# Two value projections of a fused two-block kernel in one fill of 512 weight columns each, with the packed convolution and two transposes moved around the first of them

## The reference

```python
h = rmsnorm(x, mix_pre_norm[i])
u = h @ w_in[i]
...
hv = u[..., c1 + 2 * D_RET:c1 + 3 * D_RET]
...
y_conv = conformer_conv(u_a, u_b, conv_dw_w[i], conv_dw_b[i], conv_ln_w[i], conv_ln_b[i])
y_ret = retention_group(hq, hk, hv, hg)
```

```python
kv = (mem_n @ w_kv).reshape(b, m, 2, CA_HEADS, CA_DIM)
s = jnp.einsum('bthd,bmhd->bhtm', q, kv[:, :, 0]).astype(jnp.float32)
...
o = jnp.einsum('bhtm,bmhd->bthd', p, kv[:, :, 1]).reshape(b, t, CA_WIDTH)
```

## Time and profile before

| | |
|---|---|
| median of 3 runs | 904.84 us (904.33 to 904.93) |
| profiled execution, its own time | 903.12 us |
| its span in the trace | 901.2 us |
| TensorE busy | 888.2 us, 99% of the span |
| VectorE busy | 624.2 us, 69% |
| ScalarE busy | 502.9 us, 56% |
| GpSimd busy | 347.5 us, 39% |
| granted TensorE clock, mean | 0.999 |

### The profile page before, as it was taken

One profiled execution on the slowest core, in us unless ns is written; L12 is line 12 of the kernel. 1 busy time (PEld: TensorE's weight loads), 2 busy tenths in 40 slices (PEclk: granted clock), 3 DMA queues, 4 the chain that ended last, 5 costly groups with the idle time before them and its releaser, 6 DMA issues.

```text
span 901.2 us, 15285 instructions
## 1 busy us (share of the span) xinstructions
PE 888.2 (99%) x6308; PEld 780.8 (87%) x6308; DVE 624.2 (69%) x812; ACT 502.9 (56%) x730; POOL 347.5 (39%) x133
## 2 busy tenths in 40 slices
PE   8999999999999999999999999999999999999997
PEld 7999877888888878999999988877788888888886
DVE  6999757888882267668799765753415689999623
ACT  7545646444454356655566565555545576666533
POOL 2981002666664400000000008546783166666542
PEclk9999999999999999999999999999999999999999
DMA  9762645555556545545545534444464465555551
GB/s 356 259 213 95 236 149 209 189 187 187 187 188 208 204 149 187 187 152 179 199 135 183 179 87 179 159 163 149 140 210 140 159 232 192 188 188 187 186 187 47
DMA packets 31014, 162.44 MB, mean 180 GB/s; under 512 B 9154, under 2 KB 10322, under 8 KB 12514
## 3 DMA queue, kind: packets, MB, share of 16 engines
q1 hardware_dynamic: 30738, 161.13, 51.8%
q10 hardware_dynamic: 144, 0.26, 0.1%
q0 software_dynamic: 64, 0.08, 0.0%
HBM read 160.20 MB, written 1.27 MB: 179 GB/s over the span
## 4 chain that ended last, share of the span: by engine, by line
PE 84%; DVE 9%; ACT 3%; DMA 2%; issue 1%; POOL 1%; SPq 0%; DVEq 0%; ACTq 0%
PE acc L1874 18%; PE ring L1739 15%; PE ring L2228 12%; PE ring L1773 9%; PE acc L1773 9%; PE ring L1777 5%; PE ring L1820 4%; PE acc L1777 4%; DVE acc L1281 4%; DMA raw<-wstream 2%; PE acc L2083 1%; PE acc L1887 1%; ACT w_hi L728 1%; DVE rope_b L1315 1%; DVE w_lo L1164 1%
## 5 line engine op out<-in xcount | busy, mean ns | idle before, releaser
L728 ACT CAST w_hi<-raw 128x1024 fp32r<-128x1024 f32 x284 | 297.1, 1052 | 315.4 <-PE ring L1739 78.0
L674 POOL TENSOR_TENSOR w_lo<-raw,w_hi 128x1024 fp32r<-128x1024 f32 x118 | 331.8, 2816 | 313.1 <-ACT w_hi L728 312.9
L1164 DVE TENSOR_TENSOR w_lo<-raw,w_hi 128x1024 fp32r<-128x1024 f32 x166 | 214.3, 1300 | 112.2 <-ACT w_hi L728 102.8
L1739 PE MATMUL ring<-h,w_hi 128*128 128x256 f32 x960 | 174.3, 284 | 1.0 <-issue 1.0
L1739 PEld LDWEIGHTS ring<-h,w_hi 128*128 128x128 f32 x960 | 149.8, 192 | 1.0 <-issue 0.7
L1739 PE MATMUL ring<-h,w_lo 128*128 128x256 f32 x480 | 136.1, 283 | 0.0
L1739 PEld LDWEIGHTS ring<-h,w_lo 128*128 128x128 f32 x480 | 92.2, 192 | 1.1 <-issue 1.1
L699 POOL TENSOR_SCALAR_AFFINE_SELECT toep_t<-toep_t 64x2304 f32<-64x2304 f32 x2 | 5.9, 2938 | 224.1 <-DMA toep_t<-toep 224.0
L1874 PE MATMUL acc<-w_hi,ff 128*128 128x512 f32 x340 | 91.2, 390 | 0.0
L1773 PE MATMUL ring<-h,w_hi 128*128 128x512 f32 x352 | 88.2, 393 | 0.0
L1773 PE MATMUL acc<-h,w_hi 128*128 128x512 f32 x336 | 84.6, 394 | 0.0
(11 more groups left out here) (292 smaller groups left out, 1372.2 us busy)
## 6 DMA issues: line engine op xcount, KB each, us to landing
raw<-wstream SPq DMA_DIRECT2D x142, 1024.0 KB, 4.9
toep_t<-toep SPq DMA_DIRECT2D x16, 96.0 KB, 3.1
x<-x_tok SPq DMA_DIRECT2D x2, 512.0 KB, 4.5
mem<-mem_tok SPq DMA_DIRECT2D x1, 1024.0 KB, 11.2
w_ple<-wproj SPq DMA_DIRECT2D x1, 1024.0 KB, 7.2
decay<-decay_tab SPq DMA_DIRECT2D x1, 768.0 KB, 6.4
out_t<-y SPq DMA_DIRECT2D x3, 256.0 KB, 2.1
u<-uconv SPq DMA_DIRECT2D x4, 142.0 KB, 5.8
```

What stands on the lines that cost most here:

```text
L674: nc.gpsimd.tensor_tensor(w_lo[:, u % UNITS], unit_of_raw(u), as_f32(w_hi[:, u % UNITS]), ALU.subtract).then_inc(lo_ready["pool"], 1)
L728: nc.scalar.copy(w_hi[:, u % UNITS], unit_of_raw(u)).then_inc(hi_ready, 1)
L1164: V.tensor_tensor(w_lo[:, u % UNITS], unit_of_raw(u), as_f32(w_hi[:, u % UNITS]), ALU.subtract).then_inc(lo_ready["dve"], 1)
L1739: last = mm(dst, w[a], src[:, b, kt], start=n == 0 and i == 0, stop=n == kts - 1 and i == 2)
```

## The change

Both value projections become one fill of two banks. `token_rows` takes one token tile per bank and streams 512 weight columns per matmul; the order over (token tile, k tile) is tile 0 with k 0 to 3, tile 1 with k 0 to 3, and from k 4 on both tiles for each k. The host lays the weights out by rows of four blocks for it. At the first place the packed convolution moves ahead of `v`, both memory transposes stand behind `v`, one on each side of the mean, and POOL makes `w_conv` one unit earlier. ACT reads both banks of a fill together, with one signal. At the second place the four transposes stand ahead of (0, 7) and (1, 7), and ACT reads both banks behind the transposes' casts. The number of weights, units and DMA transfers stays.

```diff
-    ("v", 0, 1, 16, "act"), ("mem_x", 0, 1, 0, "dve"), ("v", 1, 1, 16, "act"), ("mem_x", 1, 1, 0, "dve"),
+    ("v", 0, 1, 32, "act"), ("mem_x", 0, 2, 0, "dve"),
...
-    ("ple", 0, 1, 64, "acc"), ("memv", 0, 2, 16, "act"), ("ple_x", 0, 4, 0, "dve"),
+    ("ple", 0, 1, 64, "acc"), ("memv", 0, 1, 32, "act"), ("ple_x", 0, 4, 0, "dve"),
...
-    return (PJ + 1 + j,) if name == "ple_x" else (RING.index(n) % PJ,)
+    if name == "ple_x":
+        return (PJ + 1 + j,)
+    slot = sum(2 if FILLS[m][0] in ROWS else 1 for m in RING if m < n)
+    return (slot % PJ, (slot + 1) % PJ) if name in ROWS else (slot % PJ,)
...
-            feed(end_unit("v", 0))
+            feed(first_unit("v") + 1)
             pool.wait_ge(load_params, 32)
...
-            copy_fill("v", 0, v_ret[:, :, 0:256])
             for i, t in enumerate(PACKED):
                 act.wait_ge(packed_conv, i + 1)
                 A(conv_y[:, t], sc[t][:, 0:S], ACT.Identity, bias=col("dw_b", t)).then_inc(packed_out, 1)
             prime(ACT.Sqrt)
 
+            wait_fill("v", 0)
+            for tt, src in enumerate(row_banks("v", 0)):
+                ins = nc.scalar.copy(v_ret[:, tt], src)
+            ins.then_inc(freed["act"], 1)
             turned_hi("mem", 0)
-            copy_fill("v", 1, v_ret[:, :, 256:512])
             turned_hi("mem", 1)
...
-            def memv_out(j):
-                act.wait_ge(pe_step, fill_step(fi("memv", j)))
-                nc.scalar.copy(mem_v[:, :, 256 * j:256 * j + 256], bank("memv", j)[:]).then_inc(freed["act"], 1)
+            def memv_out():
+                act.wait_ge(pe_step, fill_step(fi("memv", 0)))
+                for tt, src in enumerate(row_banks("memv", 0)):
+                    ins = nc.scalar.copy(mem_v[:, tt], src)
+                ins.then_inc(freed["act"], 1)
...
-            memv_out(0)
             turned_hi("ple", 0)
             turned_hi("ple", 1)
             feed_next("ple", 5)
             turned_hi("ple", 2)
             turned_hi("ple", 3)
             feed_next("ple", 6)
-            memv_out(1)
+            memv_out()
...
+            def token_rows(name, j, src, between=None):
+
+                banks = row_banks(name, j)
+                n = fi(name, j)
+                held = {b: m for m in earlier_fills(n) for b in filled_banks(m)}
+                first = at_block[0] // UB
+                order = [(tt, kt) for tt in range(2) for kt in range(4)]
+                order += [(tt, kt) for kt in range(4, KT) for tt in range(2)]
+                for tt, kt in order:
+                    u, c = first + kt // 2, 4 * (kt % 2)
+                    if between is not None and (tt, kt) in between:
+                        between[tt, kt]()
+                    if kt == 0:
+                        m = held[filled_banks(n)[tt]]
+                        pe.wait_ge(freed[FILLS[m][3]], freed_count(m, FILLS[m][3]))
+                    if tt == 0 and c == 0:
+                        pe.wait_ge(lo_ready[LO_ENGINE[u]], lo_count(u, LO_ENGINE[u]))
+                    for part, w in ((0, w_hi), (0, w_lo), (1, w_hi)):
+                        last = mm(banks[tt], src[:, part, kt, tt * P:tt * P + P],
+                                  w[:, u % UNITS, c:c + 4].rearrange("p a b -> p (a b)"),
+                                  start=kt == 0 and part == 0 and w is w_hi, stop=kt == KT - 1 and part == 1)
+                    if tt == 1 and c:
+                        at_block[0] += UB
+                        step(last, at_block[0])
...
-            token_pair("v", 0, h)
             pe.wait_ge(w_conv_ready, len(PACKED))
             pe.wait_ge(conv_loaded, 16 * TAPS)
             for i, t in enumerate(PACKED):
                 conv_packed(i, t)
+            token_rows("v", 0, h)
             turn("mem", 0, y_tok)
-            token_pair("v", 1, h)
-            turn("mem", 1, y_tok)
             pe.wait_ge(packed_out, len(PACKED))
             pe.wait_ge(conv_ready, 1)
             for t in range(4):
                 last = mm(st[:, 0:S], mat("m512"), conv_y[:, t], start=t == 0, stop=t == 3)
             last.then_inc(stat_done, 1)
+            turn("mem", 1, y_tok)
...
-            token_pair("memv", 0, mem_n)
-            token_pair("memv", 1, mem_n, between={(1, 5): turns_of(0), (1, 7): turns_of(1)})
+            token_rows("memv", 0, mem_n, {(0, 7): turns_of(0), (1, 7): turns_of(1)})
```

More of the change, by code:

```diff
@@ L83 @@
 MERGED_BANKS = (PJ + 1, PJ + 2, 0, 1)
+ROWS = ("v", "memv")
 WIDE = ("ff", "up")
@@ L1328, in _ @@
             V.tensor_tensor(conv_y[:], conv_y[:], over(rstd[:, S:2 * S], 4), ALU.subtract).then_inc(conv_ready, 1)
-            feed_behind("v", 1)
+            feed_behind("v", 0)
             dve.wait_ge(lb_exp, 2)
@@ L2310, in host_layout @@
         add(a[j], a[4 + j])
-    add(*a[8:16], *token_blocks(w_in, (8, 9)), *a[20:24])
+    add(*a[8:16], *quarter_rows(w_in, 16), *a[20:24])
     w_kv = g["w_mem_kv_2"][0]
@@ L2319, in host_layout @@
     add(*row_blocks(g["w_ple_gate"][0]))
-    add(*token_blocks(w_kv, (2, 3)))
+    add(*quarter_rows(w_kv, 4))
     b = blocks(w_in2, range(80))
```

## The result

The changed kernel takes 913.72 us (median of 6 runs, 909.60 to 914.09) against 904.75 for the kernel before (6 runs of the same session, 904.18 to 905.25). The ratio is 1.0088, 95% interval 1.0068 to 1.0108: slower by 9.0 us, where 4.0 were forecast. Its runs scatter over 4.5 us. The profiled one took 913.67.

A forecast was written before the change was run, and what follows sets the result against it. PE and the DVE chain were both taken as limits in the first block, PE alone after the second place. Late steps of 2.45 and 1.6 us, 4.05 in sum, on the median 904.84 gave 908.8 us, range 906.3 to 911.0.

The forecast's parts named there:

- both mechanisms: Late turned memory 0 at the first place, 2.45 us, and late bank for `hq` 0 at the second, 1.6 us.
- Everything on the chain moves by 2.45 us.: First place: ACT casts turned memory 0 behind `v` and both copies, so DVE's chain to the variance runs 2.45 us later.
- That is 1.6 us more: Second place: `hq` 0 waits for the bank freed by ACT's late second copy, starting at 365.3 instead of 363.70.
- if that were all: Second place: by ACT's earlier casts alone, 0.7 us ahead, `hq` 0 would start at 363.0.
- POOL's low halves cost nothing.: First place: POOL's two later low-half casts end at 73.1, before `g` 0 at 75.9, adding no time.
- The bound of 75.6 that the rule of the port gave: First place: DVE, blocked wholly while POOL works, would still end the rotary at 75.6, ahead of 75.95.
- The matmuls, 0.6 us a place.: Either projection: 48 matmuls of 512 columns take 10.96 us against 11.5 for 96 of 256, saving 0.6 us on PE.
- rival (4), TensorE's clock: First place: the granted clock falls in the new 3 us pause, costing some 2 us, total 911; chance 0.08.
- nothing but PE's queue: Behind `hq` 0 at the second place: only PE's queue follows, PE being the limit from there on.

The follow-up runs named there:

- b_vonly: Changed kernel with only the first place's part kept; memv, its banks and reads as before the change: 906.64 us, 1.0023 of the kernel before.
- b_warm: Changed kernel with 12 and 8 idle 128-column matmuls, sized to its two new PE pauses (ahead of variance and `hq` 0): 907.84 us, 1.0035 of the kernel before.
- a_turn: Changed kernel with memory 0 turned and cast ahead of `v`, memory 1 staying behind: 907.96 us, 1.0035 of the kernel before.
- b_mend: Changed kernel with memory 0 turned ahead of `v` and the bank ring turned by one for hq, hff and hfb only: 905.22 us, 1.0009 of the kernel before.
- a_warm: Changed kernel with 28 idle 128-column matmuls ahead of the variance and 20 ahead of `hq` 0, overfilling the first pause: 913.88 us, 1.0102 of the kernel before.
- c_code: Changed kernel with 20 idle 32-column matmuls ahead of the retention's mean square, behind the first pause: 910.52 us, 1.0074 of the kernel before.
- c_best: b_mend with 10 idle 32-column matmuls ahead of the variance and 10 ahead of the retention's mean square: 903.19 us, 0.9984 of the kernel before.
- b_pad: b_mend with 48 idle 32-column matmuls near the program's start: 905.38 us, 1.0008 of the kernel before.
- c_before: Kernel before the change with 20 idle 32-column matmuls, ahead of the variance and the retention's mean square: 905.42 us, 1.0015 of the unpadded kernel.

## Why the prediction was wrong, point by point

The direction was right, as were both mechanisms; the size was off by more than a factor of two, and the time lies outside the range.

- **"Everything on the chain moves by 2.45 us."** 2.5 in the profile after, in b_vonly and in b_warm, and a_turn took it away. PE's pause was forecast as some 3 us and is 3.05. Right. DVE's wait for turned memory 0 is 7.1 us, not about 2, because the rotary of q isn't slowed; that changes nothing on the chain.
- **"That is 1.6 us more" for `hq` 0.** 1.7. In b_mend, with another bank, `hq` gains 0.6 us instead, near the 0.7 that the forecast gave for "if that were all". Right, with PE's pause 2.2 us instead of 2.5.
- **POOL's low halves cost nothing.** Right: they are under the wait, and the rotary of q is shorter than before. The bound of 75.6 that the rule of the port gave was never neared (70.4; 72.2 in b_vonly, where POOL met its last operation), since POOL came later than thought.
- **The matmuls, 0.6 us a place.** 0.230 us each in `v` of the profile after, 0.228 as read before. At the second place the gain reaches `hq` 0 (b_mend), at the first it goes into a longer wait for the variance (a_turn, 0.55 against 0.17), because DVE is the later one there.
- **The step that failed first: rival (4), TensorE's clock, at a chance of 0.08.** The forecast read from the end of the program that a pause of 3 us does not lower the clock. That reading was wrong, because the fall can come behind the pause. In the profile of before PE's last matmul ends at 895.57 and the clock falls at 899.20, 3.6 us later; in the changed kernel the first pause begins at 83.44 and the clock falls at 87.10, 3.7 us later, when PE has been at work again for 0.6 us. In four traces with a pause of 3.0 to 3.1 us ahead of the variance it fell three times, and in three with 2.2 us ahead of `hq` twice; with the waits of 3.6 and 3.8 us at the merge it fell both times. In the changed kernel's trace the two falls cost 1.1 and 1.4 us, 2.5 together, which the forecast had at nothing. The 1.1 is a net figure: as much as 0.5 us of that fall went into the wait ahead of the mean square, which is gone. With the pauses filled (a_warm, b_warm) the clock did not fall at either place. The Trainium skill's warning ("TensorE: Matmul & The Clock Gate", HAM oscillation) that idle gaps return PE to half speed had been given with the forecast and was weighed too lightly; these traces agree with it in seven of nine pauses.
- **The step that was missing: what 96 instructions fewer on PE do behind them.** The forecast had the sum of the two places and "nothing but PE's queue" behind them, and gave the removed matmuls no price but their time. The waits of "issue" rose from 1.0 to 2.9 us, and 2.5 us of the trace's loss lie where they are. c_code takes 3.2 us off with idle work alone. Even with the clock's 2.5 us the forecast would have stood at 911.3.

The sum of the steps is 2.5 + 1.7 + 1.1 + 1.4 + 2.5 = 9.2 us. The two traces differ by 10.6, of which 1.5 are the start's, and the medians by 9.0. That these agree so closely is in part luck: the profile of before lies 1.6 us below its median, that of the changed kernel at its own.

What PE waits for in the waits of "issue" is as good as shown: each of the 20 ends 1.2 to 1.6 us behind a 16 KB packet of the instruction queue, and the number of packets keeps step with that of PE's passes. That they carry PE's code is concluded from that; no row names their content. Open is why one place of the burst is covered in time and another, 40 passes on, is not, so that the waits of a new kernel can't be told ahead. Also open is the wait for POOL at the merge, 1.0 to 1.3 us in b_mend, b_vonly, c_best and c_code, which is not in the kernel before, nor in b_warm and b_pad.

## What to carry to other kernels

When a fill gets larger, ask what is read late by it: one joint read behind a long list is a late `freed` for whoever has the bank next, and one joint wait puts everything behind it in the reading engine's order behind the end of the whole fill. Price a new pause of TensorE at its length and, if it is as long as those here (2.2 us and more, seven of nine had one), at a likely fall of the clock as well; and look for that fall behind the pause, not only in it. And when an edit adds or removes instructions of TensorE, compare the waits of "issue" before and after: 20 idle matmuls gave 3.2 us in c_code and 2.0 in c_best and took 0.9 in c_before, enough to turn the verdict on a change of 1 us, so try one or two paddings before judging it.

## What the runs showed of the hardware that was not expected

- The places of the waits of "issue" depend on the number of matmul passes ahead, to within one pass, and not on the time: three waits in five kernels of 6212 passes, one in two of 6308 (and in b_pad), two in one of 6348 (c_before), none in those of 6252 (b_warm, c_best, c_code) and 6260 (b_vonly). Each ends 1.2 to 1.6 us behind a 16 KB packet of the instruction queue, which brings one for some 127 passes.
- The granted clock fell with pauses of 2.2 us in some executions, and not with one of 3.1 us in another (b_vonly). The changed kernel's runs scatter with it: 909.60 us in the run with a mean clock of 0.999, 913.67 to 914.09 in those with 0.993 to 0.995.
- A float32 matmul of 128 columns ran as two passes of 0.11 us; one of 32 columns as two passes, of which 20 took 0.75 us ahead of the variance (c_best) and 96 took 4.7 us at the start (b_pad): more than the 22 ns for each that c_best's expectation goes by.
